# Decays of the delta rule from one running sum per head, in a two-layer hybrid trunk

## The reference

```python
g = jnp.cumsum(to_chunks_s(g), axis=-1)          # running sum in a chunk, g <= 0
tril = jnp.tril(jnp.ones((CHUNK, CHUNK), bool))
strict = jnp.tril(jnp.ones((CHUNK, CHUNK), bool), -1)
decay = jnp.exp(jnp.where(tril, g[..., :, None] - g[..., None, :], -jnp.inf))
a_low = jnp.where(strict, jnp.einsum('bhncd,bhnsd->bhncs', k_beta, k) * decay, 0.0)
...                                              # solve with (a_low + 1) for u and w
attn = jnp.where(tril, jnp.einsum('bhncd,bhnsd->bhncs', q, k) * decay, 0.0)
...                                              # q_i * exp(g_i), then the scan over chunks
```

## Time and profile before

| | us |
|---|---|
| median of 3 runs | 3922.84 |
| lowest and highest | 3913.61, 3923.69 |
| the profiled execution | 3915.31 |
| its span in the trace | 3913.6 |

### The profile page before, as it was taken

One profiled execution on the slowest core, in us unless ns is written; L12 is line 12 of the kernel. 1 busy time (PEld: TensorE's weight loads), 2 busy tenths in 40 slices (PEclk: granted clock), 3 DMA queues, 4 the chain that ended last, 5 costly groups with the idle time before them and its releaser, 6 DMA issues.

```text
span 3913.6 us, 61298 instructions
## 1 busy us (share of the span) xinstructions
PE 3670.5 (94%) x19738; PEld 3126.0 (80%) x19738; DVE 2765.7 (71%) x4673; ACT 1635.0 (42%) x2982; POOL 1187.4 (30%) x800
## 2 busy tenths in 40 slices
PE   7998798899998999998999798989899999899998
PEld 4444488899998999995554387469899999899997
DVE  1623388958997888885886734168958998788886
ACT  2234234457774333333333032034445776333333
POOL 0000134585443222220443000034467444222221
PEclk8899899999999999998999899989999999999999
DMA  5553234478999999991436362224458999999995
GB/s 184 166 182 126 67 110 143 164 253 293 375 375 380 364 348 347 347 333 39 152 119 168 104 168 79 73 80 145 143 196 285 345 375 384 371 341 342 339 338 200
DMA packets 523929, 914.01 MB, mean 234 GB/s; under 512 B 70321, under 2 KB 367409, under 8 KB 515377
## 3 DMA queue, kind: packets, MB, share of 16 engines
q1 hardware_dynamic: 450096, 644.23, 48.1%
q0 software_dynamic: 73728, 268.47, 19.0%
HBM read 782.54 MB, written 130.02 MB: 233 GB/s over the span
## 4 chain that ended last, share of the span: by engine, by line
PE 40%; DVE 7%; issue 2%; DMA 2%; ACT 1%; POOL 1%; DVEq 0%; SPq 0%; ACTq 0%; POOLq 0%
PE bank L348 9%; PE bank L621 5%; PE bank L622 5%; PE bank L623 5%; PE bank L551 3%; PE bank L552 3%; PE bank L553 3%; PE bank L759 2%; PE bank L597 2%; DVE prod L2236 1%; PE bank L768 1%; DVE eq L1997 1%; DVE eq L2003 1%; DVE X L2238 1%; DVE oh L2057 1%
## 5 line engine op out<-in xcount | busy, mean ns | idle before, releaser
L551 PE MATMUL bank<-hx,hl 128*128 128x384 f32 (+1 forms) x2304 | 808.4, 351 | 61.0 <-DVE hl L1965 54.3
L552 PE MATMUL bank<-hx,hl 128*128 128x384 f32 (+1 forms) x2304 | 793.0, 344 | 0.0
L553 PE MATMUL bank<-hx,hl 128*128 128x384 f32 (+1 forms) x2304 | 792.7, 344 | 0.0
L621 PE MATMUL bank<-W,hl 128*128 128x384 f32 x2048 | 692.4, 338 | 18.1 <-DVE W L2097 17.9
L622 PE MATMUL bank<-W,hl 128*128 128x384 f32 x2048 | 691.8, 338 | 0.0
L623 PE MATMUL bank<-W,hl 128*128 128x384 f32 x2048 | 691.7, 338 | 0.0
L1264 POOL DMA_INDIRECT rows<-p_v,erow x256 | 259.4, 1013 | 830.6 <-DVE xtok L2104 788.5
L551 PEld LDWEIGHTS bank<-hx,hl 128*128 128x128 f32 x2304 | 439.9, 191 | 78.3 <-issue 61.9
L348 PE MATMUL bank<-hT,w_ring 128*128 128x512 f32 x1008 | 457.2, 610 | 45.0 <-DMA w_ring<-b_w_in 34.4
L2032 DVE SCALAR_TENSOR_TENSOR rows<-rows,xtok 128x1024 f32<-128x1024 f32 x256 | 395.9, 1584 | 102.8 <-DMA rows<-p_u,erow 102.8
L1264 POOL DMA_INDIRECT rows<-p_u,erow x256 | 353.8, 1382 | 339.9 <-DVE rows L2032 294.4
(11 more groups left out here) (293 smaller groups left out, 4993.6 us busy)
## 6 DMA issues: line engine op xcount, KB each, us to landing
w_ring<-p_u_t SPq DMA_DIRECT2D x128, 512.0 KB
hT<-p_u_t SPq DMA_DIRECT2D x128, 512.0 KB, 4.9
w_ring<-p_v SPq DMA_DIRECT2D x128, 512.0 KB
hT<-p_v SPq DMA_DIRECT2D x128, 512.0 KB, 7.0
act_scratch<-hT SPq DMA_DIRECT2D x256, 192.0 KB, 4.1
g_scratch<-gst SPq DMA_DIRECT2D x48, 1024.0 KB, 6.7
gg<-g_scratch SPq DMA_DIRECT2D x64, 768.0 KB, 7.6
ua<-act_scratch SPq DMA_DIRECT2D x256, 192.0 KB, 5.5
```

Of the source, the lines that this page charges most:

```text
L551: nc.tensor.matmul(bank[s][:, c:], hi, hx[:, 0, k, c:], start=(k == 0), stop=False)
L552: nc.tensor.matmul(bank[s][:, c:], hi, hx[:, 1, k, c:], start=False, stop=False)
L553: mm = nc.tensor.matmul(bank[s][:, c:], lo, hx[:, 0, k, c:], start=False, stop=(k == KD - 1))
L621: nc.tensor.matmul(bank[j][:, P:], hi, W[:, s, 0, :], start=first, stop=False)
```

## The change

Only one kind of product stays: the running sum of a head along the columns, in bank 2 for the first head of a round and in bank 3 for the second. The difference of two running sums is then taken by ScalarE: for each of the four blocks a Relu of the bank plus a number per partition (minus the partition's own running sum, now kept in `gtmp[:, 0]`), and one with the sign turned; an exponential with scale -1 over each of the two tiles in SBUF gives `eD` and `eDT`, and one of the bank gives `eG`. The Relu keeps the half that is masked later from growing. `SG` and its two GpSimd products a round are gone; VectorE waits for the bank of its head once, in place of one wait for each of two banks.

```diff
                 def decays(i, a):
-                    pe.wait_ge(sem("gsel_ready"), 3 * i + 3)
-                    take(2)
-                    nc.tensor.matmul(bank[2][:, :], tri[:, :], SG[:, a, :, :].rearrange("p t c -> p (t c)"),
-                                     start=True, stop=True).then_inc(psum_full[2], 1)
-                    take(3)
+                    pe.wait_ge(sem("gsel_ready"), i + 1)
+                    take(2 + a)
                     for tt in range(TT):
-                        mm = nc.tensor.matmul(bank[3][:, tt * P:(tt + 1) * P], SG[:, a, tt, :], tri[:, :],
-                                              start=True, stop=True)
-                    mm.then_inc(psum_full[3], 1)
-                    take(4)
-                    for tt in range(TT):
-                        mm = nc.tensor.matmul(bank[4][:, tt * P:(tt + 1) * P],
+                        mm = nc.tensor.matmul(bank[2 + a][:, tt * P:(tt + 1) * P],
                                               gsel[:, tt, a:a + 1].to_broadcast([P, P]), tri[:, :],
                                               start=True, stop=True)
-                    mm.then_inc(psum_full[4], 1)
+                    mm.then_inc(psum_full[2 + a], 1)
...
                 def select(i):
                     if i > 0:
-                        pool.wait_ge(psum_full[3], base[3] + 2 * i)
-                        pool.wait_ge(psum_full[4], base[4] + 3 * i - 1)
+                        pool.wait_ge(psum_full[2], base[2] + i)
+                        pool.wait_ge(psum_full[3], base[3] + i)
                     nc.gpsimd.tensor_copy(gsel[:, :, :], graw[:, :, 2 * i:2 * i + 2]).then_inc(sem("gsel_ready"), 1)
-                    for a in range(2):
-                        nc.gpsimd.tensor_tensor(SG[:, a, :, :], strict[:, :].unsqueeze(1).to_broadcast(wide),
-                                                column(graw, 2 * i + a), ALU.mult).then_inc(sem("gsel_ready"), 1)
...
                     act.wait_ge(sem("attn_raw"), 2 * i + 1)
                     act.wait_ge(sem("pack_ready"), 8 * i + 1)
-                    for b, dst in ((2, eD), (3, eDT)):
-                        full(b)
-                        nc.scalar.activation(dst[:, a, :, :].rearrange("p t c -> p (t c)"), bank[b][:, :], ACT.Exp
-                                             ).then_inc(psum_free[b], 1)
-                    full(4)
-                    nc.scalar.activation(eG[:, a, :], bank[4][:, :], ACT.Exp).then_inc(psum_free[4], 1)
+                    b, n = 2 + a, 2 * i + a
+                    full(b)
+                    for tt in range(TT):
+                        c = slice(tt * P, (tt + 1) * P)
+                        nc.scalar.activation(eD[:, a, tt, :], bank[b][:, c], ACT.Relu,
+                                             bias=gtmp[:, 0, tt, n:n + 1])
+                        ins = nc.scalar.activation(eDT[:, a, tt, :], bank[b][:, c], ACT.Relu,
+                                                   bias=gcum[:, tt, n:n + 1], scale=-1.0)
+                    step(ins)
+                    for x in (eD, eDT):
+                        flat = x[:, a, :, :].rearrange("p t c -> p (t c)")
+                        nc.scalar.activation(flat, flat, ACT.Exp, scale=-1.0)
+                    nc.scalar.activation(eG[:, a, :], bank[b][:, :], ACT.Exp).then_inc(psum_free[b], 1)
...
                 dve.sem_inc(sem("gdn_from_dve"), 1)
+                step(nc.vector.tensor_scalar(gtmp[:, 0, :, :], gcum, -1.0, None, ALU.mult))
                 dve.wait_ge(sem("gdn_from_act"), 3)
...
                     for a in range(2):
-                        dve.wait_ge(psum_free[2], t.turn(2) + 1)
+                        dve.wait_ge(psum_free[2 + a], t.turn(2 + a) + 1)
...
-                        dve.wait_ge(psum_free[3], t.turn(3) + 1)
```

More of the change, by code:

```diff
@@ L276, in hybrid_trunk @@
         gsel = sb("gsel", [P, TT, 2], where=solve_)
-        SG = sb("SG", [P, 2, TT, P], where=solve_)
         BS = sb("BS", [P, 2, TT, P], where=solve_)
```

## The result

Over five runs of each the changed kernel took 3893.0 us (3882.5 to 3896.6) where the kernel before took 3916.3 (3913.6 to 3923.7). The ratio is 0.9928, with a 95% interval of 0.9908 to 0.9947: faster by 0.7%, 28 us, with 21 to 36 us inside the interval. The means of the five differ by 28.3 us too; the medians alone differ by 23.3. The profiled execution took 3896.61 us, its span is 3894.9; it is the longest of the five runs of this kernel, and the one of before (3915.31) was shorter than four of its five, so the two spans differ by less (18.7 us) than the kernels do.

A forecast was written before the change was run, and what follows sets the result against it. TensorE was taken to bound the eight `deltanet` rounds; 28.0 us of removed products less 0 to 0.6 us for ScalarE gave a gain of 28.0 us and a forecast of 3891 us, range 3880 to 3903.

The forecast's parts named there:

- 16 x (0.86 + 0.89) = 28.0 us: TensorE, 16 heads: removed 512-column product (0.86 us) and four turned products (0.89 us) shorten a round from 37.6 to 34.1 us.
- the bounds of 0.17 and 0.40: ScalarE: range for one added Relu's price, 0.277 us less overlap up to 0.40 without overlap; worth 0 to 0.6 us altogether.
- rival 1: ScalarE: Relu missing from the exponential's or square root's table forces extra loads; gain 21 or 11 us; 0.14 with rival 2.
- its mild form: ScalarE: only the exponential's table lacks Relu; two more loads a round, 2.57 us, cost 7 us, leaving a gain of 21.
- That relief: VectorE: without GpSimd's two products beside it, the three convolution taps shorten from 3.66 to 2.32 us, about 1.3 us a round.
- Rival 2: Weight tile transfer: query tile landing in 12 us makes TensorE wait 1.7 us a round; gain 14; 0.14 with rival 1.
- 0.7 + 1.0 = 1.7 us a round altogether: ScalarE's lateness allowance: 0.7 us ahead of the query tile's copy plus VectorE's 1.0 us gap before the key tile's convolution.
- rival 3: ScalarE becomes the bound: gain gone at 0.62 us a Relu; at 0.8 us, 24 us slower, about 3942; chance 0.04.
- The sentence on the squares: TensorE at `lengths`: already waits for the key tile's squares, 2.5 us in 7 rounds, so lateness beyond the spare counts fully.
- rival 4: Key tile, copy, convolution, squares, `lengths` loop really sets the round, so nothing is gained, 3919; chance 0.02.
- The added VectorE step: VectorE at the start: 64 columns, 0.2 us, covered ahead of a product that waits 0.67 us for ScalarE.
- The starting point: Kernel time before: profiled execution 3915.31 us gives 3887.3, three-run median 3922.84 gives 3894.8; forecast put between, at 3891.

The follow-up runs named there:

- the test with bank 4: Changed kernel with eight more Relus a head and the second value tile's transposes in bank 4, not 5: rounds of 35.83 us, ratio to before 0.9958.

## Why the prediction was right

**The term that carries it.** 16 x (0.86 + 0.89) = 28.0 us; the run times give 28, but with 21 to 36 in the interval, so the test of this term is the round: 34.1 against 34.10. Over the whole stretch, from the first `lengths` to the last transpose, the chain was 294.0 us (1835.53 to 2129.55) and is 266.3 (1841.47 to 2107.73), 27.8 less. The products put back give 37.6 again, so nothing else had a share that could be seen. Reading the price from the chain and not from the matmul rows mattered: by the earlier trace rows the instructions add up to 54 us, since neighbours overlap.

**ScalarE.** The Relus start 0.25 us apart, where 0.29 was taken, inside the bounds of 0.17 and 0.40. The second head ends 16.0 us into the round (1959.46 + 0.58), where 16.6 was worked out, and the idle time ahead of the query tile's copy is 1.3, not 0.7. ScalarE loads a table three times a round, as before, and the second head's Relus run behind exponentials with no load between, so rival 1 was void; forced, its mild form cost 9 us where 7 was worked out, again for the smaller spare.

**VectorE and GpSimd.** VectorE's gap ahead of the query tile's convolution went from 2.66 to 0.49 us (0.5 was forecast), the one ahead of the key tile's stayed at 1.00, and the three taps of `conv(i,3)` take 2.33 us where they took 3.66. That relief is worth nothing, as forecast.

**Transfers.** The slowest of the weight loads landed in 7.2 us; TensorE waited for none. Rival 2 didn't happen.

**The step that was wrong without harm.** "0.7 + 1.0 = 1.7 us a round altogether" counted VectorE's gap ahead of the key tile as spare. It lies behind the point where TensorE waits for bank 5, which the prediction never looked at; for `take` it checked banks 2 and 3 only. The real spare was ScalarE's 1.3 and some 0.2 at the bank, 1.5. The sum of the two errors is small because ScalarE's part was underrated by 0.6 us and VectorE's overrated by 0.8: that 1.7 is near 1.5 is luck. The narrow place could have been read from the trace of the kernel before, where the product that frees bank 5 ends at 1940.73 and the transpose starts at 1941.08 (timeline, then chain):

```profile
1940.04 0.69 DVE L2207 TENSOR_TENSOR pack<-bank,gstat 128x512 f32<-128x512 f32 x1 [0.24 <-DVE pack L2199]
...
1941.08 0.44 PE bank L699 x4
```

The wrong spare did no harm, because the Relus used up none of it. It shows in rival 3: there the prediction has the kernel level with before at 0.62 us a Relu. Measured, it is level already at 4.0 us more in a round, 16 x 0.25, an effective 0.50 us a Relu, and at 0.75 it is 0.85% slower than before, 33 us (23 to 43), where that reckoning gives 17. By the traces the difference is bank 5 and the lower clock behind its gap; the test with bank 4 was made at the first of these two points only.

**The sentence on the squares.** "`lengths` already waits a little" took a wait of the weight load for a wait of the product. There was none, as the run that moved them shows, and the edge that rival 4 starts from wasn't there either.

**Start and end.** The added VectorE step took 0.20 us, and VectorE still waited 0.40 us for ScalarE behind it, so it is covered as forecast. In the profiled executions the changed kernel comes to the first `lengths` 5.9 us later than before, and takes 3.1 us more behind the rounds; with the 27.8 us of the rounds that is the 18.7 between the spans. Neither is seen to come from the change: ScalarE's last table load ahead of the delta rule, in code that wasn't touched, is already 8.5 us later (1795.24 for 1786.77), and the stretch behind the rounds, 1784.1 and 1787.2 us, goes from 1774.9 to 1790.8 in the other runs.

**The starting point.** Taken between the profiled execution and the median of three, about 3919, it gave 3891; the median came out at 3893.0. That it is so near is in part luck: the median of the kernel before, of five runs now, is 3916.3, 3 us lower than the start, and the medians differ by 23.3 us, 5 less than the term.

## What to carry to other kernels

Where the chain that ended last runs over one engine for a whole round, take the price of removed work from that chain's own pieces, and walk through the others in their order to see how late each may be. In that walk a gap is spare only if no wait of the bounding engine lies ahead of it; so list every bank and buffer that the bounding engine takes in the round, with who frees it and when, not only those of the edit. A bank that is shared by two tiles of one round can be the next bound while every engine still shows idle time: here 3.4 us less TensorE a round gained nothing, and one spare bank gave back half of what a late ScalarE cost (1.7 us a round longer in place of 3.5).

## What the hardware showed beyond that

- Relus of 128 columns from PSUM, with a number per partition as bias, start 0.25 us apart, though each is shown as 0.35 to 0.42 us long, longer from one to the next in a series.
- Two gaps of TensorE of 2.31 us in neighbouring rounds, alike in the trace, were followed by a product of 7.03 and one of 8.46 us, at a granted clock of 1.00 and 0.84. A wait of the busiest engine cost up to 1.7 us on top of itself (rounds of 36.6 and 38.3). Behind the gaps of 1.02 us (two table loads more) and of 1.50 us (bank 4) no product was slower; behind those of 6.43 us (sixteen more Relus) every one was, 8.03 to 9.19 us.
- Four fp32 transposes of 128 x 128 take 0.44 us in the chain, four fp32 products of that size 0.89. A transpose is one instruction there (x4) and a product two (x8), so both come to 0.11 us an instruction.
